# Hybrid decoder on one Trainium2 core: both pairs of down blocks by seven products, evicted by ScalarE and added by DMA

## The reference, cut to what matters

```python
def conv_gated_ffn(x, w_up, conv_w, conv_b, w_down):      # D_FF = 5632
    gu = x @ w_up                                          # (256, 2 * 5632)
    gate, up = gu[..., :D_FF], gu[..., D_FF:]
    gate = causal_depthwise_conv(gate, conv_w, conv_b)     # 3 taps along the tokens
    return (jax.nn.silu(gate) * up) @ w_down               # (256, 2048)

for i in range(DEPTH):                                     # 2 layers
    ...
    h = h + conv_gated_ffn(rms_norm(h, norm_ffn_g[i]), w_up[i], conv_w[i], conv_b[i], w_down[i])
    gate = jax.nn.sigmoid(rms_norm(h, norm_ple_g[i]) @ w_ple_gate[i])
    h = h + (p[i] @ w_ple[i]) * gate
```

## Time and profile before

| | us |
|---|---|
| median of 3 runs | 2156.09 (2156.04 to 2156.51) |
| the profiled execution's own time | 2156.12 |
| its span | 2154.3 |
| TensorE busy | 2141.7 |
| VectorE busy | 1707.6 |
| ScalarE busy | 1125.1 |
| GpSimd (POOL) busy | 50.4 |

### The profile page before, as it was taken

How to read it: one execution, slowest core, us unless ns; L and a number is a source line. 1 busy time by engine, 2 the same in 40 slices (tenths; PEclk the granted TensorE clock), 3 DMA queues, 4 the chain that set the end, 5 groups by cost and what they waited for, 6 DMA issues and landing times.

```text
span 2154.3 us, 32719 instructions
## 1 busy us (share of the span) xinstructions
PE 2141.7 (99%) x11526; PEld 1859.3 (86%) x11526; DVE 1707.6 (79%) x2192; ACT 1125.1 (52%) x1422; POOL 50.4 (2%) x114
## 2 busy tenths in 40 slices
PE   9999999999999999999999999999999999999998
PEld 8898888888888888888898988888888888888886
DVE  5797569888889888897557875788888889888964
ACT  6556445554555544555554664445544545544554
POOL 2000000000000000000000000000000000000011
PEclk9999999999999999999999999999999999999999
DMA  8645555546555546555556455555556555556562
GB/s 269 213 139 174 178 200 188 182 158 233 205 204 178 182 166 234 197 192 195 173 183 182 138 176 176 201 203 176 186 177 234 195 197 176 183 185 234 176 216 97
DMA packets 233323, 406.75 MB, mean 189 GB/s; under 512 B 14828, under 2 KB 50268, under 8 KB 233096
## 3 DMA queue, kind: packets, MB, share of 16 engines
q1 hardware_dynamic: 231976, 402.72, 55.0%
q0 software_dynamic: 512, 1.76, 0.2%
q10 hardware_dynamic: 736, 1.07, 0.1%
HBM read 403.42 MB, written 2.10 MB: 188 GB/s over the span
## 4 chain that ended last, share of the span: by engine, by line
PE 97%; ACT 1%; DVE 1%; issue 1%; POOL 0%; POOLq 0%; DVEq 0%; ACTq 0%
PE acc L2082 16%; PE tps L2082 16%; PE acc L1901 12%; PE acc L1903 12%; PE acc L1902 12%; PE tps L2092 9%; PE acc L2092 9%; PE tps L1902 3%; PE tps L1903 3%; PE tps L1901 3%; PE acc L1988 1%; PE tps L1958 1%; ACT sq_h L773 0%; DVE h L1536 0%; DVE xb_lo L1193 0%
## 5 line engine op out<-in xcount | busy, mean ns | idle before, releaser
L996 ACT ACTIVATE w_hi<-raw 128x1024 fp32r<-128x1024 f32 x540 | 559.2, 1058 | 536.3 <-PE acc L2092 116.6
L1566 DVE TENSOR_TENSOR w_lo<-raw,w_hi 128x1024 fp32r<-128x1024 f32 x540 | 650.2, 1225 | 161.5 <-ACT w_hi L996 149.8
L1181 DVE TENSOR_TENSOR w_lo<-raw,w_hi 128x1024 fp32r<-128x1024 f32 (+1 forms) x288 | 342.0, 1211 | 143.2 <-ACT w_hi L722 137.6
L722 ACT ACTIVATE w_hi<-raw 128x1024 fp32r<-128x1024 f32 (+2 forms) x287 | 290.2, 1044 | 179.5 <-PE acc L1903 126.3
L2082 PE MATMUL acc<-xa,w_hi 128*128 128x512 f32 x1536 | 366.0, 391 | 0.0
L2082 PE MATMUL tps<-xa,w_hi 128*128 128x512 f32 x1536 | 361.2, 390 | 0.0
L2082 PEld LDWEIGHTS tps<-xa,w_hi 128*128 128x128 f32 x1536 | 285.3, 188 | 57.2
L2082 PEld LDWEIGHTS acc<-xa,w_hi 128*128 128x128 f32 x1536 | 283.7, 188 | 56.2 <-DVE h L1521 0.4
L1902 PE MATMUL acc<-w_hi,xb_lo 128*128 128x512 f32 x640 | 249.0, 389 | 0.0
L1901 PE MATMUL acc<-w_hi,xb_hi 128*128 128x512 f32 x560 | 220.5, 394 | 0.4 <-ACT pw L1072 0.4
L1903 PE MATMUL acc<-w_lo,xb_hi 128*128 128x512 f32 x560 | 218.1, 389 | 0.0
(11 more groups left out here) (262 smaller groups left out, 2651.1 us busy)
## 6 DMA issues: line engine op xcount, KB each, us to landing
raw<-in_w_up SPq DMA_DIRECT2D x176, 1024.0 KB, 5.0
raw<-in_w_down SPq DMA_DIRECT2D x88, 1024.0 KB, 5.0
raw<-in_w_out SPq DMA_DIRECT2D x32, 1024.0 KB, 5.0
raw<-in_w_ple_gate SPq DMA_DIRECT2D x32, 1024.0 KB, 5.1
raw<-in_w_in SPq DMA_DIRECT2D x21, 1024.0 KB, 5.4
raw<-in_w_ukv SPq DMA_DIRECT2D x8, 1024.0 KB, 5.5
raw<-in_w_in SPq DMA_DIRECT2D x8, 864.0 KB, 4.8
raw<-in_w_uq SPq DMA_DIRECT2D x6, 1024.0 KB, 5.7
```

Of the source, the lines that this page charges most:

```text
L722: copy(w_hi[:, half_of(m), 0:n], raw[:, c % RAW_SLOTS, at:at + n], ACT.Copy).then_inc(hi_done, 1)
L996: copy(w_hi[:, half_of(m), :], raw[:, c % RAW_SLOTS, half * HALF:(half + 1) * HALF], ACT.Copy).then_inc(hi_done, 1)
L1181: dve.tensor_tensor(w_lo[:, half_of(m), 0:n], raw[:, c % RAW_SLOTS, at:at + n], w_hi[:, half_of(m), 0:n].bitcast(F32), ALU.subtract).then_ ...
L1566: dve.tensor_tensor(w_lo[:, half_of(m), :], raw[:, slot, half * HALF:(half + 1) * HALF], w_hi[:, half_of(m), :].bitcast(F32), ALU.subtract ...
```

## The change: both pairs of blocks by seven products

A unit is cut into two phases of 15 halves: eight gate halves and seven products (blocks 0 and 1, into the banks of `tps`), then eight up halves and seven products (blocks 2 and 3, into the banks of `acc`). A unit has 30 halves instead of 27. The pieces are loaded in that order: four of w_up, two of w_down, and the same again. Each w_down piece serves three or four of the seven products, so its slot of `raw` is free only after T2 or T4 is split.

No product is added by VectorE any more. ScalarE copies each bank to `stage` (`take`), scaled where it goes into `h`, and GpSimd issues a DMA that adds it (`accum_op`) to a running sum or to `h`; `stage` may be written again when all seven of a phase have landed (`stage_free`). The fifth to seventh products use banks of the first to third, so TensorE waits for those copies (`staged`); the first half of each phase (`BY_BANK`) takes the banks in the order in which they come free: 3, 0, 1, and 2 after six matmuls.

Tap 2 moves from VectorE to ScalarE (`tap_2`, with scale and bias columns). Up's lo copy, its sum and `gated` move to the start of the next unit. The loop has nine turns of one unit, and the last unit is written out, with its own order (`ends`). There are two sets of running sums; the first set's corner sums stand in the last unit, and blocks 0 and 1 too get their kept sums in `add_block`. The last unit's g is split by VectorE and not by POOL.

```diff
 # TensorE, one unit
-                    by_rows(m0, gate_bank(b0, w), 0, 8, w)
-                    by_rows(m0 + 8, up_bank(j0, w), 0, 8, w)
...
+                    for i in range(8):
+                        x_half(i, i, gate_acc, v)
+                    pe.wait_ge(t_done, JOBS * l + JOB_UNIT * v + (j0 + T_BANKS))
                     pe.wait_ge(g_lo, UNITS * l + u)
-                    free_acc(l, b0 + 2, w)
-                    corner_product(m0 + FORM_B11, w, a11, acc[0][:, 0, :])
-                    corner_product(m0 + FORM_B21, w, a12, acc[0][:, 1, :])
+                    product(0, B11, tps[:, 0, :])
+                    product(0, B21, tps[:, 1, :])
                     pe.wait_ge(s_split_lo, (UNITS - 1) * l + u)
...
-                    for _ in down(m0 + PLAIN_0, b0 + 4, gt, w):
-                        pass
-                    for _ in down(m0 + PLAIN_1, None, gt, w, j0 + 7):
-                        pass
+                    product(0, B22, tps[:, 2, :])
+                    product(0, T1, tps[:, 3, :])
+                    pe.wait_ge(staged, taken(l, v, 0, 1))
+                    product(0, T3, tps[:, 0, :])
+                    pe.wait_ge(staged, taken(l, v, 0, 2))
+                    product(0, T2, tps[:, 1, :])
+                    pe.wait_ge(staged, taken(l, v, 0, 3))
+                    product(0, T4, tps[:, 2, :])
+                    for i in range(8):
+                        x_half(PHASE + i, i, up_acc, v)
+                    block_split(l, b0, v)
+                    block_split(l, b0 + 1, v)
+                    product(1, B11, acc[0][:, 0, :])
...
 # ScalarE
+                    def take(second, k, bank, scale=1.0):
+                        halves_used(act, l, M_UNIT + PHASE * second + FORM_AT + k, v)
+                        if k == B11:
+                            act.wait_ge(stage_free, phases(l, v, second))
+                        copy(stage[:, k, :], bank, ACT.Copy, scale=scale).then_inc(staged, 1)
...
+                    go(5, 10)
+                    take(0, B11, tps[:, 0, :])
+                    go(10, 11)
+                    take(0, B21, tps[:, 1, :], rstd["ffn"][:, 0:1])
...
+                    go(14, 15)
+                    take(0, T2, tps[:, 1, :])
+                    gate_low(lambda: halves_used(act, l, M_UNIT + 7, v))
+                    take(0, T4, tps[:, 2, :], rstd["ffn"][:, 1:2])
+                    go(15, 17)
+                    tap_2(u)
...
 # GpSimd
+                def products_added(v, second):
+                    p1, p7, p6, p5 = sums[second]
+                    j = 2 * second
+                    for i, dst in enumerate((p1, h[:, 0, j * BLK:(j + 1) * BLK], h[:, 0, (j + 1) * BLK:(j + 2) * BLK], p5, p7, p6,
+                                            h[:, 1, j * BLK:(j + 1) * BLK])):
+                        pool.wait_ge(staged, taken(l, v, second, i + 1))
+                        pool.sem_inc(stage_seen, 1)
+                        pool.dma_start(dst, stage[:, i, :], accum_op=ALU.add).then_inc(added, 16)
+                    pool.wait_ge(added, 16 * TAKES * phases(l, v, second))
+                    pool.sem_inc(stage_free, 1)
...
 # VectorE, one unit
-                    go(17, 19)
-                    dve.wait_ge(corners_zero, 2 * l + 2)
-                    product_added(FORM_B11, sum_p1, acc[0][:, 0, :], None, acc_free[0])
-                    product_added(FORM_B21, h_block(0, 2), acc[0][:, 1, :], 0, acc_free[0])
...
+                    go(0, 1)
+                    up_sum(u - 1)
+                    gated(u - 1)
+                    go(1, 3)
+                    s_sums(v, 0)
+                    s_sums(v, 1)
...
+                    go(4, 5)
+                    t_sum(v, 0, 1)
+                    t_sum(v, 0, 2)
...
+                    go(19, 20)
+                    if ends:
+                        corners_summed(0, 0)
+                        corners_summed(0, 1)
+                    t_sum(v, 1, 1)
+                    t_sum(v, 1, 2)
...
 # VectorE, end of the layer
                     if j < 2:
-                        add_block(l, bd + j, j)
+                        p1, p7, p6, p5 = sums[0]
+                        add_block(l, bd + j, j, ((p1, p7), (p6, p5))[j])
```

More of the change, by code:

```diff
@@ L50 @@
 T_BANKS = 4
-ACC_UNIT = 6
-JOB_UNIT = 12
-TURN_UNITS = 2
+ACC_UNIT = 2
+JOB_UNIT = 4
 CORNERS = 7
+TAKES = 7
 ROWS_JOBS = 5
@@ L1051, in _ @@
+                    go(27, 28)
+                    take(1, T1, acc[1][:, 1, :])
+                    go(28, 29)
+                    take(1, T3, tps[:, 0, :])
+                    go(29, 30)
+                    take(1, T2, tps[:, 1, :])
+                    take(1, T4, tps[:, 2, :], rstd["ffn"][:, 1:2])
+                first_unit()
+                with act.Fori(1, UNITS - 1) as u:
+                    unit(u, u - 1, False)
+                unit(UNITS - 1, UNITS - 2, True)
                 d0 = M_DOWN
@@ L1566, in split_u, with t_sum @@
                     dve.tensor_tensor(w_lo[:, half_of(m), :], raw[:, slot, half * HALF:(half + 1) * HALF],
                                       w_hi[:, half_of(m), :].bitcast(F32), ALU.subtract).then_inc(lo_done, 1)
-                def corner(i, k, half):
-                    slot = (CH["ffn"] + 4 * (KT // 4) + i * UNIT_CHUNKS + k) % RAW_SLOTS
-                    return raw[:, slot, half * HALF:(half + 1) * HALF]
-                def t_sum(w, i, k, dst, a, b):
+                def t_sum(v, second, k):
+                    c = CH["ffn"] + 2 * (KT // 4) + PHASE_CHUNKS * second
+                    b11, b21, b12, b22 = (raw[:, (c + Q_CHUNK[q]) % RAW_SLOTS, a * HALF:(a + 1) * HALF]
+                                          for q in range(2) for a in range(2))
+                    c += Q_CHUNK[1]
@@ L1754, in unit @@
                     go(26, 27)
+                    go(27, 30)
                 first_unit()
[L1757 to L1768 removed]
+                with dve.Fori(1, UNITS - 1) as u:
+                    unit(u, u - 1, False)
@@ L2409, in _ @@
+                    pe.wait_ge(t_done, JOBS * l + (JB["p"] + T_BANKS))
+                    product(1, T3, tps[:, 0, :])
+                    product(1, T2, tps[:, 1, :])
+                    product(1, T4, tps[:, 2, :])
                 jobs_split(l, JB["ffn_norm"] + 5)
                 first_unit()
-                with pe.Fori(0, LOOPS) as w:
-                    for i in range(TURN_UNITS):
-                        unit(w, i)
+                with pe.Fori(1, UNITS - 1) as u:
+                    unit(u, u - 1, False)
```

463 lines of the change are left out of this document (265 added, 198 removed).

## The result

The changed kernel takes 2288.48 us (median, 2286.78 to 2290.51) against 2156.24 of the kernel before: ratio 1.061, 95% interval 1.0595 to 1.0632. It is slower by 132 us; the forecast of 2146 and its whole range (2130 to 2176) were wrong, and the time is 114 us above rival B's, the one with the right sign and the right cause.

A forecast was written before the change was run, and what follows sets the result against it. The prediction took TensorE, busy 2141.7 of 2154.3 us, as the bound: matmuls times their pitch. It summed 2156.1 - 27.2 (matmuls) + 7 (ScalarE) + 4 (load chain) + 6 (layer ends) = 2146 us, range 2130 to 2176.

The forecast's parts named there:

- rival B: Accumulating DMAs cost twice a plain one, so loads land some 2.9 us later instead of 1.2: 2174 us; chance 0.22.
- six fewer matmuls: TensorE's down products: 2 x 42 matmuls a unit instead of 42 and 48, 20 times: 27.2 us gained.
- ScalarE late at bank 2: First short stage: TensorE waits 0.35 us a unit for ScalarE's evictions, splits and gate copies: 7 us.
- last unit of a layer: Corner sums, up sum and gate product, 5.8 us more VectorE work, fall where it has 8.5 free: nothing.
- ends of layers, VectorE's extra adds: Two more VectorE adds each before blocks 0 and 1 are transposed: 2.95 us a layer, 6 for two.
- load chain: From a load to the second short stage: accumulating DMAs beside loads cost 0.2 us a unit beyond the room: 4 us.
- The price: An accumulating DMA costs what a plain transfer does, 0.77 us of all sixteen engines; from above 1.54.
- The load and its company: Four accumulating DMAs beside a load of the next phase's third or fourth piece delay it by some 1.2 us.
- The room: From load issue to B11's eviction in the second short stage: 22.1 us of work before 23.8, leaving 1 us.
- A: No wait at all: ScalarE enters early, loads land in time, VectorE's lead hides the layer's end: 2129 us; chance 0.16.
- C: POOL issuing a DMA holds VectorE's two-operand instructions, 2.3 us a unit or more: 2192 us; chance 0.05.

The follow-up runs named there:

- e2: Changed kernel with the fourteen transfers of a unit from `stage` and the wait for their landing left out, so the products' sums are not computed: 2155.49 us.
- e6: Changed kernel without transfers from `stage` (sums left out), and ScalarE evicts T4 ahead of its two gate copies: 2146.7 us.
- e10: Changed kernel with GpSimd adding the fourteen products of a unit itself by `tensor_tensor` instead of issuing adding transfers: 2366.01 us.
- e9: Changed kernel, five additions held, T4 earlier, corner sums and ScalarE's end wait moved, own semaphore for first two transfers, ScalarE's g split behind B22: 2148.58 us.

## Why the prediction was wrong, point by point

| term | forecast | measured | from |
|---|---|---|---|
| six fewer matmuls | -27 | -27 | 11406 matmuls |
| ScalarE late at bank 2 | +7 | +11 | e2, gone in e6 |
| last unit of a layer | 0 | +10 | e2 less before up to p's transposes: -6.2, where the two terms above give -16 |
| ends of layers, VectorE's extra adds | +6 | +5 | e2: 30.2 us instead of 27.7 from p's transposes to block 3's, twice |
| load chain | +4 | +115 | e2 to after, up to p's transposes: 58.2 and 56.6 a layer |
| additions at the ends | in the one above | +21 | e2 to after, from there on: 9.9 and 11.5 |

From 2156.2 they sum to 2291; the profiled run, from which they are read, took 2290.5. The first four rows are read from the kernel without transfers, the last two are what the additions put on top of it.

**The load chain is the step that failed**, in three places. *The price*: "I take this end, as the nearest row", a plain transfer's 0.77 us. It is 1.45; the upper bound of 1.54 was right and was put aside. *The load and its company*: "four of them beside a load delay it by some 1.2 us". The forecast followed the third and fourth w_up pieces, whose slots T2 and T4 free; the two w_down loads behind them, which feed the t-sums and the products, it did not follow. In the changed kernel the last w_up piece and the two w_down pieces were issued at 715.80, 718.09 and 720.33, one behind the other on one queue, and landed after 13.3, 14.9 and 15.2 us. By the trace's packets, two of the phase's seven additions ran before that (713 to 716.3), and five from 720.0 to 730.3, in equal turns with these loads, which so got some 66 packets a microsecond instead of 200. Five additions are 5 x 1.41 = 7.0 us of the DMA engines (an estimate from their 128 packets of 176 ns), most of the 8.4 us by which the w_down load came later than without them (15.3 and 6.9); even plain copies made it 4.3. Rival B had the price, but still one load with 2.9 us of delay, so it gave 2174. *The room*: "1 us". For a w_down load it is 12.4 - 6.9 = 5.5. I put gate sums, norm and taps behind the load; the chain from landing to landing doesn't contain them, and of VectorE's work it holds eleven splits and four t-sums. This error has the other sign and so hid a part of the first two.

One thing in this stays open. Between 716.4 and 720.0 no addition ran, though the third had been issued at 715.04 and the loads left room (125, 168 and 108 packets in the three microseconds from 717 on). In nearly all phases of the loop its packets began 5.0 to 5.3 us after its issue, within 0.3 us of VectorE's next pause; the first two began 1.4 us after theirs, in the middle of VectorE's row of splits. Whether VectorE's work held GpSimd's later transfers back was not tested; had they run at once, fewer would have stood beside the w_down loads.

**ScalarE at bank 2**: right in place and cause. The view's idle time was 0.3 us, as computed; by the distance of starts (0.68 instead of 0.23) it was 0.45. The matmul behind a wait starts its successor 0.33 us later instead of 0.23, so each wait costs 0.1 more than its idle time, and this one 0.56. With six waits a unit after the change, this is 0.6 us a unit.

**The last unit** was costed at nothing since VectorE had 8.5 us free in a unit. The average was true (VectorE 55.98 us in a unit of the changed kernel against 55.0 forecast, ScalarE 43.82 against 46.6), but the 5.8 us of extra work stand in a row ahead of splits that TensorE takes next: without transfers TensorE waited 1.5 us there for up_sum, 1.0 for w_lo and 0.7 for a `stage` copy of ScalarE (distances of starts, less 0.23).

**The ends**: right where VectorE's adds are the cause. ScalarE's wait for the last seven landings (7.3 and 8.0 us, since xb_hi lies where `stage` did) was in the code shown and had no term at all.

**The rivals.** A: without the additions and with T4 ahead the time is still 2147, so no wait at all was never near. B was the mechanism, with the price about right: 1.45 us an addition against 0.66 a copy. C didn't come: VectorE's splits beside GpSimd's DMA rows stayed at 1.22 us, and in e10, where GpSimd reads SBUF, they took 2.10. Both are as the rule says that the prediction took for C from the Trainium skill, "SBUF — State Buffer" (Who interferes with whom).

## What to carry to other kernels

Follow a load from its issue through what it feeds to the release of its slot: landing plus the rest of that loop is a period of its own, and its room is found only by what truly waits in it. A DMA that adds has two prices, its own engine time (here 1.9 times a load's per byte) and the turns it takes from every load in flight; count all that can stand beside the load and beside the loads ahead of it on its queue, not the average share. The place of the additions mattered more here than their number: with five of each seven held until the w_down loads had landed, 133 us became 3.

## What the runs showed of the hardware

- Adding transfers within SBUF, 256 KB: 128 packets of 2 KB at 176 ns; copying ones: 64 packets of 4 KB at 159 ns (medians). Adding packets of 1 KB: 101 ns.
- Two queues with work took equal turns by packet, though the packets cost 176 and 84 ns: some 62 packets of additions and 68 of loads a microsecond, 98 and 200 alone (all seven held).
- An adding transfer of GpSimd began 1.4 us after its issue, or up to 5.2 us after it with the DMA engines partly idle (changed kernel); the cause is not shown.
- After an idle time of 3.4 us TensorE's granted clock was 0.51 (1.2 GHz) for some 3.4 us, eight matmuls at some 0.43 us instead of 0.23 (e9); after 3.0 us it was 0.50 too (changed kernel, 993.4 to 996.0); a single wait of 1.65 us in the changed kernel was followed by rows at full length.
